# Taking the constant products out of the norm pauses of a two-block transformer kernel

## The chip, the cores and the metric

The kernel runs as one launch on one NeuronCore of a Trainium2 chip. The metric is the device time of the launch in microseconds (us); lower is better. TensorE (PE in the profile) does the matrix products, VectorE (DVE) and ScalarE (ACT) the elementwise work, GpSimd (POOL) and SyncE (SP) mostly start transfers.

## The reference

Two blocks of a network are run one after the other on 256 tokens of width 1024, all in float32.

The first block has two layers over a context and a latent sequence of 256 tokens each (512 columns together). Layer 0 is a retention mixer, layer 1 a differential attention mixer; each is followed by a gated feed-forward part of hidden width 2816. In front of every mixer and feed-forward part stands a modulated RMS norm:

```
def modulate(x, shift, scale):
    return rms_norm(x) * (1.0 + scale) + shift
```

The second block has two layers over the latent tokens. Each has a feed-forward part of hidden width 4096, a mixer with three branches (a gated delta rule and two kinds of chunked attention), and another feed-forward part; after each of the three stands a LayerNorm:

```
x = layer_norm(alpha * x + 0.5 * swiglu_2(x, w_ff1_in[l], w_ff1_out[l]), ln1_g[l], ln1_b[l])
...
x = layer_norm(alpha * x + mix, ln2_g[l], ln2_b[l])
x = layer_norm(alpha * x + 0.5 * swiglu_2(x, w_ff2_in[l], w_ff2_out[l]), ln3_g[l], ln3_b[l])
```

## The kernel before

**Products.** Every weight matrix is cut into tiles of 1 MB (16 blocks of 128x128). SP loads them through a ring of four buffers `raw`; ACT makes a rounded copy `w_hi` of each tile (ring of two), DVE the rest `w_lo`, in place of `raw`. Activations are split the same way. One float32 product is then three matmuls (high by high, high by low, low by high), in `product` (L444 to L446) and `product_rows` (L450 to L452). `wide_both` does it with two (L500 with 512 columns, L501 with 256). PE waits for `lo_done` at each tile and counts `tile_used` at its end; that count lets ACT and DVE go on with the tile after the next.

**Order of the work.** Each engine runs a program written out by hand, in order. The engines meet at semaphores only: an engine stands still at `wait_ge` until another has counted far enough.

**The pauses of the norms.** Between the last product of one part and the first product of the next lies a norm, and it needs the sum over all 1024 features. There are nine such pauses in which TensorE has constant products to do:

- Pause A, ahead of the first feed-forward part: sums of squares on TensorE (L601, L593), then ACT and DVE scale and split eight blocks of features, one after the other. `wide(..., blocks=...)` starts the next part block by block, as `block_ready` counts them.
- Pause B, ahead of the differential attention; the same, with 256 columns first.
- Pause C, ahead of the second feed-forward part; the same.
- Pause D, ahead of the second block: the residual is added and split, without a norm.
- Pauses E, five of them, in `turned_norm(n)` for n = 0 to 4 (the two layers have n % 3 = 0, 1, 2; the last norm of all doesn't go through TensorE). The tokens lie on the partitions there. DVE and ACT work out mean and deviation of the first 128 tokens, PE turns them with eight transposes (L642), then the same for the other 128 (L649); DVE and ACT scale and split the eight blocks, and the next part starts with block 0.

**The constant products.** `keep_clock(bank_, count)` issues `count` float32 matmuls of a matrix of ones with four constant 128x128 matrices, 512 columns each, into a PSUM bank that nothing reads before it is written anew. The profile has two instructions for each of them (L440). There are 1 and 5 in pause A, 4 in B, 4 in C, 4 in D, and 3, 1 and 1 in each pause E: ahead of the first transposes, between the two groups, and behind the second. They wait for nothing of their own. Those behind a `wait_ge` stand in order behind it.

Of the kernel before, what the change touches and what calls it, by code (L numbers as in the profile page):

```python
# [32 lines left out]
P = 128  # L33
# [60 lines left out]
def build(nc, ws, xt, col1, row1, col2, row2, relb, cst, ret_cst, ret_dist, c64, crow, aw, lnrow, out):  # L94
# [3 lines left out]
    def at(name, shape, kb, dtype=F32):  # L98
        return nc.alloc_sbuf_tensor_at(name, shape, dtype, offset=base + int(kb * KB) // 32 * 32)
# [13 lines left out]
    cs = at("cs", [P, 6, P], 96)  # L113
    ident, ones, ones64, rot_ret, rot_diff, swap64 = (cs[:, i, :] for i in range(6))
# [121 lines left out]
    with ExitStack() as ctx:  # L236
        ps = ctx.enter_context(nc.psum_tensor("ps", [P, 8, 512], F32))
# [62 lines left out]
        def tiles(phase, layer, eng, body, first=0, count=None, per=4):  # L300


            n0, _, total = PH[phase]
            count = total - first if count is None else count
            turns = count // per
            done = 0
            if turns > 1:
                with eng.Fori(0, turns) as i:
                    for u in range(per):
                        body(i, u, n0 + first + u, i * (per // 4) + layer * (NL // 4))  # L310
                done = turns * per
            for u in range(done, count):
                body(0, u, n0 + first + u, layer * (NL // 4))
# [9 lines left out]
        UNITS = [("q", 0), ("q", 1), ("ka", 0), ("kb", 0), ("ka", 1), ("kb", 1), ("va", 0), ("vb", 0), ("q", 2), ("ka", 2), ("kb", 2),  # L323
                 ("va", 1), ("vb", 1), ("q", 3), ("ka", 3), ("kb", 3), ("va", 2), ("vb", 2), ("va", 3), ("vb", 3)]
        UNIT_TILE = list(itertools.accumulate(0 if n == 0 or kind[1:] == "b" else 1 for n, (kind, _) in enumerate(UNITS)))
        DIFF_OUT_BANK = (0, 0, 1, 1, 4, 4, 5, 5)

# [102 lines left out]
        def _(pe):  # L430
            mm = nc.tensor.matmul

            def pass_wait():

                pe.sem_inc(waits_passed)

            def keep_clock(bank_, count):

                for _ in range(count):
                    mm(ps[:, bank_, :].rearrange("p (a b) -> p a b", b=P), ones, cs[:, 0:4, :], start=True, stop=True)  # L440

            def product(out_, blk, s, rhs_hi, rhs_lo, start, stop):

                mm(out_, w_hi[:, s % SPLIT, blk], rhs_hi, start=start, stop=False)  # L444
                mm(out_, w_hi[:, s % SPLIT, blk], rhs_lo, start=False, stop=False)  # L445
                return mm(out_, w_lo[:, raw_slot(s), blk], rhs_hi, start=False, stop=stop)  # L446
# [42 lines left out]
            def wide_both(phase, layer, rhs, first=0, count=None, blocks=None):  # L489

                def body(i, u, s, turn):
                    wait_tile(s, turn)
                    pe.wait_ge(sums_taken, group(phase, layer, i * 4 + first + u - 1))
                    for n in range(2 * DC):
                        c, mi = (n // 2, n % 2) if blocks is not None else (n % DC, n // DC)
                        if blocks is not None and mi == 0:
                            pe.wait_ge(block_ready, blocks + c + 1)
                            pass_wait()
                        o, blk = ps[:, ring(first + u) + mi, :], mi * DC + c
                        mm(o.rearrange("p (a b) -> p a b", b=T), w_hi[:, s % SPLIT, blk], rhs[:, :, c, :], start=c == 0, stop=False)  # L500
                        ins = mm(o[:, 0:T], w_lo[:, raw_slot(s), blk], rhs[:, 0, c, :], start=False, stop=c == DC - 1)  # L501
                    ins.then_inc(tile_used, 1)
                if blocks is not None:
                    pe.wait_ge(sums_taken, group(phase, layer, first + 2))
                    pass_wait()
                tiles(phase, layer, pe, body, first, count)
# [18 lines left out]
            def deep(phase, layer, rhs_hi, rhs_lo, width, parts, complete, early=None):  # L525


                def body(i, u, s, turn):
                    wait_tile(s, turn)
                    q = u % parts  # L530
                    if q == 0:
                        pe.wait_ge(sums_taken, group(phase, layer, u // parts + 1))
                    if u == parts - 1:
                        pe.wait_ge(operand_ready, complete)
                        pass_wait()
                    b = pair(phase, u // parts)
                    for mi in range(2):
                        if mi and early is not None:
                            early(u)
                        for c in range(DC):  # L540
                            ins = product(ps[:, b + mi, 0:width], mi * DC + c, s, rhs_hi[:, q * DC + c, :],
                                          rhs_lo[:, q * DC + c, :], q == 0 and c == 0, q == parts - 1 and c == DC - 1)
                    ins.then_inc(tile_used, 1)
                tiles(phase, layer, pe, body, per=4 * parts)
# [42 lines left out]
            def squares(q, cols, some, sq, bank_=5):  # L587

                width = cols.stop - cols.start
                for c in some:  # L590
                    pe.wait_ge(sq_ready, q * DC + c + 1)
                    pass_wait()
                    ins = mm(ps[:, bank_, 0:width], ones, sq[:, c, 0:width], start=c == 0, stop=c == DC - 1)  # L593
                if c == DC - 1:
                    ins.then_inc(square_sum, 1)

            def added_squares(q, width, sq, number):

                pe.wait_ge(sq_added, number)
                pass_wait()  # L600
                mm(ps[:, 5, 0:width], ones, sq[:, 0, 0:width], start=True, stop=False)  # L601
# [33 lines left out]

            def turned_norm(n):

                keep_clock(0 if n % 3 == 1 else 5, 3)
                pe.wait_ge(z_ready, n * 3 + 1)
                pass_wait()  # L640
                for c in range(DC):
                    nc.tensor.transpose(ps[:, 4 + 2 * (c % 2), (c // 2) * P:(c // 2 + 1) * P], x_tok[:, 0, c * P:c * P + P], ident)  # L642
                for c in (0, 2, 4, 6, 1, 3, 5, 7):
                    if c == 0:
                        keep_clock(5, 1)
                    if c < 2:
                        pe.wait_ge(z_ready, n * 3 + 2 + c)
                        pass_wait()
                    ins = nc.tensor.transpose(ps[:, 5 + 2 * (c % 2), (c // 2) * P:(c // 2 + 1) * P], x_tok[:, 1, c * P:c * P + P],  # L649
                                              ident)  # L650
                    if c in (6, 7):
                        ins.then_inc(z_turned, 1)
                keep_clock(3, 1)

            pe.sem_inc(tile_used, SPLIT)

# [77 lines left out]
            for j in range(16):  # L734
# [6 lines left out]
                for n, (kb, ka) in enumerate(keys):  # L741
                    ins = mm(ps[:, HO_BANK[j], :], att[:, h % 2, ka, (q % 2) * P:(q % 2) * P + P], V[:, h, kb, :],  # L742
                             start=n == 0, stop=n == len(keys) - 1)
# [6 lines left out]
            pe.wait_ge(ho_copied, 12)  # L750
            wide("ret_g", 0, h_hi, h_lo, TT, early=lambda u: (head_turned(14), head_turned(15)) if u == 0 else None)
            deep("ret_out", 0, y_hi, y_lo, TT, 2, 2)
            keep_clock(6, 1)
            added_squares(1, TT, SQ_RET, 1)
            squares(1, slice(0, TT), range(6, DC), SQ_RET)
            keep_clock(6, 5)
            wide("ffn_in0", 0, h_hi, h_lo, TT, 0, 4, blocks=DC)
            pe.wait_ge(operand_ready, 3)
            wide("ffn_in0", 0, h_hi, h_lo, TT, 4)
# [1 line left out]


            squares(2, slice(0, TT), range(5, DC), SQ_DIFF, 0)
            keep_clock(6, 4)

            def projection():

# [232 lines left out]
                    if j > 7:  # L1000
                        squares(3, LAT, (j // 2 - 5, j // 2 - 4), SQ_LAT, 7)
            squares(3, LAT, range(4, DC), SQ_LAT, 7)
            keep_clock(6, 4)
            wide_both("ffn_in1", 0, h_both[:, :, :, LAT], 0, 1, blocks=3 * DC)
            pe.wait_ge(operand_ready, 7)
            wide_both("ffn_in1", 0, h_both[:, :, :, LAT], 1, 1)
            wide_both("ffn_in1", 0, h_both[:, :, :, LAT], 2)
            ffn_out("ffn_out1", slice(0, T), 8)
            pe.wait_ge(x_ready, DC + 1)
            keep_clock(0, 4)  # L1010


            for layer in range(LAYERS2):
# [14 lines left out]
                wide_both("ff1_in", layer, l_both, 4)  # L1028
                ff_out("ff1_out", "ff1_in", layer, layer * 7 + 10)
                turned_norm(layer * 3)  # L1030
                wide("w_in", layer, l_hi, l_lo, T, 0, 4, blocks=layer * 3 * DC + 5 * DC)
                have(2)
# [165 lines left out]
                for lv in range(6):  # L1198
                    for g in range(2):
                        pe.wait_ge(inv_ready, layer * 12 + lv * 2 + g + 1)  # L1200
                        pass_wait()
                        for y, half, h, n in systems(range(4 * g, 4 * g + 4)):
                            rhs = TU[half, g, 0, y % 4, :] if lv else m64[half, 9, :]
                            ins = mm(ps[half, 4 + 3 * g, (y % 4) * CH:(y % 4 + 1) * CH], Mm[half, y, :], rhs,
                                     start=True, stop=True)
                        ins.then_inc(inv_p, 1)
                    products(3)
                    for g in range(2):
# [4 lines left out]
                        for y, half, h, n in systems(range(4 * g, 4 * g + 4)):  # L1213
                            p, u, at_ = Pm[half, y, :], TU[half, g, 1, y % 4, :], y % 4
# [17 lines left out]
                for y, half, h, n in systems(range(8)):  # L1232
                    ins = mm(ps[:, 4 + h // 2, y * CH:y * CH + CH], kbg[half, y, :], TU[half, y // 4, 1, y % 4, :],
                             start=True, stop=True)
# [3 lines left out]
                for n in range(4):  # L1238
                    if n:
                        pe.wait_ge(sc_next, layer * 3 + n)  # L1240
                        pass_wait()
                        for j, hp, half, h in heads:
                            ins = mm(ps[half, 2, j * P:j * P + P], wT[:, 8 * hp + 4 * j + n, :], Sst[:, n % 2, h, :],
                                     start=True, stop=True)
# [4 lines left out]
                    if n < 3:  # L1249
                        for j, hp, half, h in heads:  # L1250
                            ins = mm(ps[:, 6 + hp, j * P:j * P + P], kdec[half, 4 * j + n, :], vnew[half, n % 2, j, :],
                                     start=True, stop=True)
# [4 lines left out]
                    for j in range(2):  # L1257
                        outs = [ps[:, 3 + 2 * hp, j * T + n * CH:j * T + n * CH + CH] for hp in range(2)]
                        for hp, half in enumerate(HALVES):
                            if n:  # L1260
                                mm(outs[hp], Sst[:, n % 2, 2 * hp + j, :], qdec[:, 8 * hp + 4 * j + n, :],
                                   start=True, stop=False)
                        for hp, half in enumerate(HALVES):
                            ins = mm(outs[hp], vnew[half, n % 2, j, :], qkT[half, 4 * j + n, :],
                                     start=n == 0, stop=True)
# [1880 lines left out]
```

## Time and profile before

| | |
|---|---|
| median of 3 runs | 2979.86 us (2979.3 to 2986.58) |
| time of the profiled execution | 2979.24 us |
| its span, first to last instruction | 2977.4 us |
| PE busy | 2922.7 us, 98% |
| weight loads on PE | 2486.7 us, 84% |
| DVE busy | 1978.0 us, 66% |
| ACT busy | 1269.8 us, 43% |
| mean granted TensorE clock | 0.999 of full speed |

Busy times are sums over the instructions of an engine. A matmul's record reaches a little beyond the start of the next one, since matmuls are pipelined; how fast they follow each other is read from their starts. The granted clock is given as a share of 2.4 GHz: 1.00 is 2.4 GHz and 0.50 is 1.2 GHz.

### The profile page before, as it was taken

The numbers are of one execution on the slowest core, as the hardware profiler recorded it, in microseconds if no ns is written. First come the engines' busy times: TensorE is split into PE (matmuls) and PEld (weight loads), VectorE is DVE, ScalarE is ACT, GpSimd is POOL, SyncE is SP. The second block draws the span as 40 slices with busy tenths as digits, with TensorE's granted clock in tenths as the row PEclk, the third lists the DMA queues.
The fourth block names the chain that finished last, engine by engine and source line by source line (L and its number), as shares of the span: only waits on it lengthen the run. The fifth ranks groups of instructions, "written<-read, shape, count | busy, mean of one in ns | idle before, by whom it ended". The sixth has DMA issues, their size and how long they took to land.

```text
span 2977.4 us, 45013 instructions
## 1 busy us (share of the span) xinstructions
PE 2922.7 (98%) x17734; PEld 2486.7 (84%) x17734; DVE 1978.0 (66%) x2717; ACT 1269.8 (43%) x1469; POOL 25.0 (1%) x36
## 2 busy tenths in 40 slices
PE   8999999999999999999999999999999999999998
PEld 5896887888877788988889988888888899988887
DVE  5754656766656767477557867775677478777764
ACT  5312224222154465344443635554544345536553
POOL 0000000000000000010000000000100000000000
PEclk9999999999999999999999999999999999999999
DMA  7430343444522145455545324555555544335554
GB/s 296 156 128 15 134 149 134 163 170 161 191 90 71 57 144 195 169 199 194 200 171 183 143 86 162 188 187 185 184 192 188 210 160 169 104 138 180 187 183 169
DMA packets 71595, 475.35 MB, mean 160 GB/s; under 512 B 8065, under 2 KB 8225, under 8 KB 19745
## 3 DMA queue, kind: packets, MB, share of 16 engines
q1 hardware_dynamic: 57744, 418.47, 39.2%
q10 hardware_dynamic: 11520, 41.95, 4.2%
q0 software_dynamic: 2192, 12.96, 1.1%
q8 instruction: 102, 1.67, 0.2%
q14 instruction: 37, 0.30, 0.0%
HBM read 472.31 MB, written 1.05 MB: 159 GB/s over the span
## 4 chain that ended last, share of the span: by engine, by line
PE 91%; DVE 5%; ACT 2%; DVEq 1%; issue 1%; DMA 0%; ACTq 0%; SPq 0%
PE ps L500 18%; PE ps L444 12%; PE ps L445 12%; PE ps L446 12%; PE ps L501 9%; PE ps L450 6%; PE ps L451 6%; PE ps L452 6%; DVE w_lo L1878 2%; PE ps L742 1%; PE ps L712 1%; PE ps L440 1%; PE ps L816 1%; ACT w_hi L1314 0%; DMA raw<-in_ws 0%
## 5 line engine op out<-in xcount | busy, mean ns | idle before, releaser
L1878 DVE TENSOR_TENSOR w_lo<-raw,w_hi 128x2048 fp32r<-128x2048 f32 x369 | 846.0, 2293 | 497.1 <-ACT w_hi L1314 495.5
L1314 ACT CAST w_hi<-raw 128x2048 fp32r<-128x2048 f32 x367 | 700.5, 1909 | 658.4 <-PE ps L446 325.0
L500 PE MATMUL ps<-l_both,w_hi 128*128 128x512 f32 x2048 | 718.5, 396 | 4.4 <-DVE small L2053 2.4
L501 PE MATMUL ps<-l_both,w_lo 128*128 128x256 f32 x2048 | 572.7, 280 | 0.0
L500 PEld LDWEIGHTS ps<-l_both,w_hi 128*128 128x128 f32 x2048 | 384.1, 188 | 100.4 <-issue 6.5
L501 PEld LDWEIGHTS ps<-l_both,w_lo 128*128 128x128 f32 x2048 | 386.4, 189 | 0.0
L444 PE MATMUL ps<-h_both,w_hi 128*128 128x512 f32 (+1 forms) x736 | 285.8, 388 | 3.4 <-DVE h_both L2142 2.1
L446 PE MATMUL ps<-h_both,w_lo 128*128 128x512 f32 (+1 forms) x736 | 279.8, 380 | 0.0
L445 PE MATMUL ps<-h_both,w_hi 128*128 128x512 f32 (+1 forms) x736 | 279.7, 380 | 0.0
L444 PE MATMUL ps<-l_both,w_hi 128*128 128x256 f32 x848 | 247.7, 292 | 2.7 <-DVE w_lo L1932 1.2
L1435 ACT COPY low_part<-ps 128x512 f32<-128x512 f32 x150 | 88.1, 587 | 369.5 <-PE ps L501 369.5
L446 PE MATMUL ps<-l_both,w_lo 128*128 128x256 f32 x848 | 239.8, 283 | 0.0
L445 PE MATMUL ps<-l_both,w_hi 128*128 128x256 f32 x848 | 239.8, 283 | 0.0
L450 PE MATMUL ps<-w_hi,fh_hi 128*128 128x512 f32 x512 | 199.2, 389 | 0.0
L452 PE MATMUL ps<-w_hi,fh_lo 128*128 128x512 f32 x512 | 199.2, 389 | 0.0
L451 PE MATMUL ps<-w_lo,fh_hi 128*128 128x512 f32 x512 | 199.2, 389 | 0.0
L444 PEld LDWEIGHTS ps<-h_both,w_hi 128*128 128x128 f32 x736 | 138.3, 188 | 39.2 <-issue 12.3
L444 PEld LDWEIGHTS ps<-l_both,w_hi 128*128 128x128 f32 x848 | 162.3, 191 | 10.4 <-issue 6.1
L445 PEld LDWEIGHTS ps<-l_both,w_hi 128*128 128x128 f32 x848 | 162.4, 192 | 0.6 <-issue 0.5
L446 PEld LDWEIGHTS ps<-l_both,w_lo 128*128 128x128 f32 x848 | 162.3, 191 | 0.0
L445 PEld LDWEIGHTS ps<-h_both,w_hi 128*128 128x128 f32 x736 | 138.4, 188 | 26.8 <-issue 1.7
L446 PEld LDWEIGHTS ps<-h_both,w_lo 128*128 128x128 f32 x736 | 138.3, 188 | 26.5
(468 smaller groups left out, 5006.3 us busy)
## 6 DMA issues: line engine op xcount, KB each, us to landing
raw<-in_ws SPq DMA_DIRECT2D x396, 1024.0 KB, 4.8
aT<-in_aw ACTq DMA_DIRECT2D x80, 512.0 KB, 4.1
ln_rows<-in_lnrow POOLq DMA_DIRECT2D x4, 1024.0 KB, 6.1
X<-in_xt SPq DMA_DIRECT2D x1, 2048.0 KB, 11.2
dist<-in_ret_dist POOLq DMA_DIRECT2D x1, 2048.0 KB, 14.8
relB<-in_relb POOLq DMA_DIRECT2D x2, 768.0 KB, 7.3
c_rows<-in_crow POOLq DMA_DIRECT2D x1, 1024.0 KB, 9.0
last_rows<-in_lnrow POOLq DMA_DIRECT2D x1, 1024.0 KB, 5.9
```

What stands on the lines that cost most here:

```text
L440: mm(ps[:, bank_, :].rearrange("p (a b) -> p a b", b=P), ones, cs[:, 0:4, :], start=True, stop=True)
L444: mm(out_, w_hi[:, s % SPLIT, blk], rhs_hi, start=start, stop=False)
L445: mm(out_, w_hi[:, s % SPLIT, blk], rhs_lo, start=False, stop=False)
L446: return mm(out_, w_lo[:, raw_slot(s), blk], rhs_hi, start=False, stop=stop)
L450: mm(out_, x_hi, w_hi[:, s % SPLIT, blk], start=start, stop=False)
L451: mm(out_, x_hi, w_lo[:, raw_slot(s), blk], start=False, stop=False)
L452: return mm(out_, x_lo, w_hi[:, s % SPLIT, blk], start=False, stop=stop)
L500: mm(o.rearrange("p (a b) -> p a b", b=T), w_hi[:, s % SPLIT, blk], rhs[:, :, c, :], start=c == 0, stop=False)
L501: ins = mm(o[:, 0:T], w_lo[:, raw_slot(s), blk], rhs[:, 0, c, :], start=False, stop=c == DC - 1)
L1314: nc.scalar.copy(w_hi[:, s % SPLIT], raw[:, raw_slot(s)]).then_inc(hi_done, 1)
L1435: nc.scalar.copy(low_part[:, own], ps[:, b:b + 2, T:TT]).then_inc(low_ready, 1)
L1878: tt(w_lo[:, raw_slot(s)], raw[:, raw_slot(s)], w_hi[:, s % SPLIT].bitcast(F32), ALU.subtract).then_inc(lo_done, 1)
```

## The change

All calls of `keep_clock` go, and the function with them. Nothing is put in their place; all waits, all other instructions and their order stay.

```diff
--- before.py
+++ after.py
@@ -434,11 +434,6 @@
 
                 pe.sem_inc(waits_passed)
 
-            def keep_clock(bank_, count):
-
-                for _ in range(count):
-                    mm(ps[:, bank_, :].rearrange("p (a b) -> p a b", b=P), ones, cs[:, 0:4, :], start=True, stop=True)
-
             def product(out_, blk, s, rhs_hi, rhs_lo, start, stop):
 
                 mm(out_, w_hi[:, s % SPLIT, blk], rhs_hi, start=start, stop=False)
@@ -635,14 +630,11 @@
 
             def turned_norm(n):
 
-                keep_clock(0 if n % 3 == 1 else 5, 3)
                 pe.wait_ge(z_ready, n * 3 + 1)
                 pass_wait()
                 for c in range(DC):
                     nc.tensor.transpose(ps[:, 4 + 2 * (c % 2), (c // 2) * P:(c // 2 + 1) * P], x_tok[:, 0, c * P:c * P + P], ident)
                 for c in (0, 2, 4, 6, 1, 3, 5, 7):
-                    if c == 0:
-                        keep_clock(5, 1)
                     if c < 2:
                         pe.wait_ge(z_ready, n * 3 + 2 + c)
                         pass_wait()
@@ -650,7 +642,6 @@
                                               ident)
                     if c in (6, 7):
                         ins.then_inc(z_turned, 1)
-                keep_clock(3, 1)
 
             pe.sem_inc(tile_used, SPLIT)
 
@@ -750,10 +741,8 @@
             pe.wait_ge(ho_copied, 12)
             wide("ret_g", 0, h_hi, h_lo, TT, early=lambda u: (head_turned(14), head_turned(15)) if u == 0 else None)
             deep("ret_out", 0, y_hi, y_lo, TT, 2, 2)
-            keep_clock(6, 1)
             added_squares(1, TT, SQ_RET, 1)
             squares(1, slice(0, TT), range(6, DC), SQ_RET)
-            keep_clock(6, 5)
             wide("ffn_in0", 0, h_hi, h_lo, TT, 0, 4, blocks=DC)
             pe.wait_ge(operand_ready, 3)
             wide("ffn_in0", 0, h_hi, h_lo, TT, 4)
@@ -761,7 +750,6 @@
 
 
             squares(2, slice(0, TT), range(5, DC), SQ_DIFF, 0)
-            keep_clock(6, 4)
 
             def projection():
 
@@ -1000,14 +988,12 @@
                     if j > 7:
                         squares(3, LAT, (j // 2 - 5, j // 2 - 4), SQ_LAT, 7)
             squares(3, LAT, range(4, DC), SQ_LAT, 7)
-            keep_clock(6, 4)
             wide_both("ffn_in1", 0, h_both[:, :, :, LAT], 0, 1, blocks=3 * DC)
             pe.wait_ge(operand_ready, 7)
             wide_both("ffn_in1", 0, h_both[:, :, :, LAT], 1, 1)
             wide_both("ffn_in1", 0, h_both[:, :, :, LAT], 2)
             ffn_out("ffn_out1", slice(0, T), 8)
             pe.wait_ge(x_ready, DC + 1)
-            keep_clock(0, 4)
 
 
             for layer in range(LAYERS2):
```

## Rows read from the trace of the kernel before

**Rows 1.** The page: busy times, granted clock, and the shares of the last-ending chain.

```profile
PE 2922.7 (98%) x17734; PEld 2486.7 (84%) x17734; DVE 1978.0 (66%) x2717; ACT 1269.8 (43%) x1469; POOL 25.0 (1%) x36
...
PEclk9999999999999999999999999999999999999999
...
PE 91%; DVE 5%; ACT 2%; DVEq 1%; issue 1%; DMA 0%; ACTq 0%; SPq 0%
```

**Rows 2.** The constants' line: duration in ns (min/median/max), first and last start.

```profile
L440 PE MATMUL ps<-cs x86: 590/592/596, 471.6 to 2696.9; 128*128 128x512 f32 x86
```

**Rows 3.** Timeline of PE, pause A and its last two blocks (start, us, instructions).

```profile
471.58 1.02 PE L440 MATMUL ps<-cs 128*128 128x512 f32 x2
472.44 1.02 PE L601 MATMUL ps<-SQ_RET,cs 128*128 128x512 f32 x2
474.25 1.95 PE L593 MATMUL ps<-SQ_RET,cs 128*128 128x512 f32 x4 [0.79 <-ACT SQ_RET L1340]
476.04 4.45 PE L440 MATMUL ps<-cs 128*128 128x512 f32 x10
481.20 0.47 PE L444 MATMUL ps<-h_both,w_hi 128*128 128x512 f32 x1 [0.70 <-DVE h_both L1939]
...
491.17 0.47 PE L444 MATMUL ps<-h_both,w_hi 128*128 128x512 f32 x1
...
492.39 0.39 PE L446 MATMUL ps<-h_both,w_lo 128*128 128x512 f32 x1
492.85 0.47 PE L444 MATMUL ps<-h_both,w_hi 128*128 128x512 f32 x1
```

**Rows 4.** Timeline of PE, pause B.

```profile
850.23 3.60 PE L440 MATMUL ps<-cs 128*128 128x512 f32 x8
853.96 0.36 PE L444 MATMUL ps<-h_both,w_hi 128*128 128x256 f32 x1
```

**Rows 5.** Timeline of PE, pause C.

```profile
1068.86 3.60 PE L440 MATMUL ps<-cs 128*128 128x512 f32 x8
1073.63 0.47 PE L500 MATMUL ps<-h_both,w_hi 128*128 128x512 f32 x1 [1.17 <-DVE h_both L1939]
```

**Rows 6.** Timeline of PE, pause D.

```profile
1265.01 3.60 PE L440 MATMUL ps<-cs 128*128 128x512 f32 x8
1269.26 0.47 PE L500 MATMUL ps<-l_both,w_hi 128*128 128x512 f32 x1 [0.65 <-DVE l_both L2564]
```

**Rows 7.** Timeline of PE, the first of the five pauses E.

```profile
1535.95 2.73 PE L440 MATMUL ps<-cs 128*128 128x512 f32 x6
1538.70 1.06 PE L642 MATMUL ps<-cs,x_tok 128*128 128x128 f32 x8
1539.60 1.02 PE L440 MATMUL ps<-cs 128*128 128x512 f32 x2
1540.66 1.08 PE L649 MATMUL ps<-cs,x_tok 128*128 128x128 f32 x8
1541.59 1.02 PE L440 MATMUL ps<-cs 128*128 128x512 f32 x2
1543.00 0.36 PE L444 MATMUL ps<-l_both,w_hi 128*128 128x256 f32 x1 [0.39 <-DVE l_both L2034]
```

**Rows 8.** Timeline of DVE in that pause: what frees PE.

```profile
1537.74 0.81 DVE L1998 TENSOR_SCALAR x_tok<-x_tok,negmu,inv_std 128x1024 f32<-128x1024 f32 x1 [0.24 <-ACT inv_std L1378]
...
1539.97 1.00 DVE L2020 TENSOR_SCALAR x_tok<-x_tok,negmu,inv_std 128x512 f32<-128x512 f32 x2 [0.64 <-ACT inv_std L1388]
1541.34 0.54 DVE L2026 TENSOR_SCALAR X<-ps,cols 128x256 f32<-128x256 f32 x1 [0.36 <-PE ps L649]
```

**Rows 9.** Timeline of PE at the second tile behind pauses E, n = 0.

```profile
1549.58 0.39 PE L444 MATMUL ps<-l_both,w_hi 128*128 128x256 f32 x1 [0.59 <-DVE w_lo L1932]
```

**Rows 10.** The same for n = 1.

```profile
1852.10 0.48 PE L500 MATMUL ps<-l_both,w_hi 128*128 128x512 f32 x1 [1.21 <-DVE small L2053]
```

**Rows 11.** Timeline of PE at the kernel's start: one form of matmul.

```profile
6.59 4.35 PE L678 MATMUL ps<-raw,cond_raw 128*4 128x256 f32 x10 [6.59 <-DMA raw<-in_ws]
...
10.38 1.86 PE L678 MATMUL ps<-raw,cond_raw 128*4 128x256 f32 x7
15.47 1.89 PE L678 MATMUL ps<-raw,cond_raw 128*4 128x256 f32 x8 [3.23 <-DMA raw<-in_ws]
17.30 0.60 PE L663 MATMUL ps<-parts_sum,ada_row 4*128 4x2 f32 x4
```

**Rows 12.** Stretches: length, each engine's busy us (instructions), granted clock, DMA.

```profile
10.00:15.00 5.00, 2.24 (x9) 0.66 (x7) 1.25 (x3) 2.06 (x4) 0.00 (x0) 1.00 0.99 420
...
2967.80:2970.00 2.20, 0.00 (x0) 0.00 (x0) 2.07 (x4) 1.57 (x5) 0.00 (x0) 1.00 0.00 0
2970.20:2972.00 1.80, 0.00 (x0) 0.00 (x0) 1.65 (x5) 0.50 (x2) 0.00 (x0) 0.50 0.00 0
```

**Rows 13.** Timeline of PE: its last matmul.

```profile
2967.34 0.39 PE L452 MATMUL ps<-w_hi,fh_lo 128*128 128x512 f32 x1
```

## The prediction

> **What bounds the kernel now.** I read the page first. TensorE is busy for 98% of the span and makes up 91% of the chain that ended last, and its granted clock reads 9 (90% or more) in all forty slices [rows 1]. So the kernel is bound by TensorE at full clock, and whatever slows the products there goes into the time nearly one for one. Next I asked for the line of the constants: 86 instructions, 590 to 596 ns each, spread from 471.6 to 2696.9 us [rows 2]. Then I read the timeline of PE around each of their places. In pause A the ten instructions of the second call start at 476.04 and the next follows 4.45/10, about 0.43 us, behind each; the 86 fill some 37 us of TensorE. The question is only whether these 37 us stand in for idle time, and what idle time would do instead. Last I looked for places where TensorE's clock changes without the constants: only the two ends of the kernel have such rows.
>
> **What goes.** 43 calls, 86 instructions. Each stands ahead of a wait that ends later than they do. Pause A: they run from 476.04 to 480.5 and the next product starts at 481.20, when DVE has released it (0.70 us idle left) [rows 3]; pause C leaves 1.17 us [rows 5], pause D 0.65 [rows 6]. Pause B has the least room, but the row behind it shows the product at 853.96, 0.13 us behind the end of the last constant's record [rows 4]; its operand came at about that time. In pause E the first transpose starts at 1538.70, and DVE wrote its operand until 1537.74 + 0.81 = 1538.55; the second group starts at 1540.66, and half of the 1.00 us of DVE's two instructions that began at 1539.97 ends at 1540.5 [rows 7, 8]. So in both places TensorE starts 0.15 us behind the operand, constants or not. The cover of the whole edit is this: the norm's chain on ACT and DVE, which has nothing to do with the constants. Taking them out gives back nothing directly. Bounds: at best 0.15 us at each of ten transpose groups and at pause B, 1.6 us; at worst a start from standstill is later. The first product of pause C comes 0.26 us behind its block, as do those of A and D, against 0.15 in E, so a loss of 0.1 at six places, 0.6 us. I take 0.4 us of loss.
>
> **What is idle then.** Pause A: 472.5 to 474.25, and 476.0 to 481.20 (5.2 us) [rows 3]. B: 850.2 to 853.96 (3.7 us) [rows 4]. C: 4.8 us [rows 5]. D: 4.3 us [rows 6]. E: 2.75 us, eight transposes (0.9 us), 1.06 us, eight transposes, 1.4 us [rows 7]; that is 5.2 idle of 7.05, five times over.
>
> **What the clock does in idle time.** The end of the kernel shows it: the last matmul starts at 2967.34 and its record ends at 2967.73 [rows 13]; the granted clock is 1.00 until 2970.00 and 0.50 from 2970.20 on [rows 12]. So 2.4 us behind the last product the clock was at 1.2 GHz. Against that, TensorE was idle for 3.23 us up to 15.47 and the clock stayed at 1.00 [rows 11, 12]. So idle time of this size sometimes brings the clock down and sometimes not; pauses A, C and D are longer than either, B is a little longer, and E is made of pieces around it. I take it that the clock falls in A, C and D, nearly always in B, and in most of the five E.
>
> **What a fallen clock costs.** The start shows both levels for one form of matmul. The first ten start from 6.59 to 10.38, 3.79/9 = 0.42 us apart; the eight from 15.47 to 17.30 are 1.83/8 = 0.23 us apart [rows 11]. At the low level work takes 1.84 times as long, so each us of it loses 0.46 us. There the high level came at about 10.7, some 4.1 us behind the first matmul. If a pause's products run that long at 1.2 GHz, it loses 4.1 x 0.46 = 1.9 us. But the fall comes during the pause, and part of the low stretch lies in idle time; then half, 0.95 us, is left. Between the two I take 1.4 us, since the products start only when the norm is over and the low stretch has to last into them.
>
> **What of it is absorbed.** Behind A, B and C the blocks arrive more slowly than PE takes them. In A a block comes every 492.85 - 491.17 = 1.68 us, and its work ends at 492.39 + 0.23, 1.45 us after its start [rows 3]: 0.23 us to spare in each of seven, 1.6 us in all. For B and C I take 1.1 and 1.4 us from the same blocks at 256 columns (0.16 and 0.20 each). D has no such room. E with n = 0 and 3 waits 0.59 us for the second tile's weights [rows 9], n = 1 and 4 wait 1.21 us [rows 10], n = 2 doesn't wait. These waits are for ACT's and DVE's work on tiles that TensorE has released earlier, so they don't move with it.
>
> Loss less absorption, with 1.4 us a pause: A 0, B 0.3, C 0, D 1.4, E 0.8 x 2 + 0.2 x 2 + 1.4 = 3.4. Sum 5.1 us. With 1.9 us: A 0.3, B 0.8, C 0.5, D 1.9, E 1.3 x 2 + 0.7 x 2 + 1.9 = 5.9. Sum 9.4. With 0.95 us: D 0.95, E 0.35 x 2 + 0.95 = 1.65. Sum 2.6.
>
> **Transposes at the low clock.** The chain of E runs through TensorE: DVE starts on block 0 at 1541.34, 0.7 us behind the first transpose of the second group [rows 7, 8], after four of its eight. Eight take 0.9 us; four take 0.45, and at the low clock 0.38 more. That is late for all that follows, for nothing is absorbed ahead of it: 5 x 0.38 = 1.9 us if the clock falls before them each time, 0 if never. I take half, 1.0 us.
>
> On this the Trainium skill has a rule that speaks against my middle value (TensorE: Matmul & The Clock Gate, Part 4: PE-mode transpose): full speed doesn't engage for transposes as it does for other matmuls. No run here shows it yet; by it each E would be one pause of 7.05 us and the clock would fall ahead of the second group every time, and the sum would be the third rival's.
>
> **Sum.** 5.1 + 1.0 + 0.4 = 6.5 us. The profiled execution took 2979.24 us, 1.84 more than its span; it lies 0.6 us below the median of the runs. 2979.24 + 6.5 = 2985.7; with half of the distance to the median, 2986. That is 0.2%, and a measurement of this kernel tells about 0.3%, 8.9 us, from no change.
>
> **Rivals.**
>
> First, the clock falls in most pauses and the loss is partly absorbed: my forecast, 2982 to 2988.8. Chance 0.47.
>
> Second, the clock doesn't fall, or only where it costs nothing. The 3.23 us of idleness at full clock [rows 11, 12] speak for it, the last 2.4 us [rows 12, 13] against. Time: 2979.9. Chance 0.11.
>
> Third, the transposes don't hold the clock up, and all five E run from their first transposes into their products at 1.2 GHz. E costs 5.9 + 1.9 us, A to D 1.7 (0.3 and 1.4, as above), the slower starts 0.6: 10.1 us, 2989.3, and so slower. For it: 5.2 of 7.05 us are idle in each E. Against it: only 2.75 us lie in one piece. It decides from the point at which the five E together cost more than 6.5 us. Chance 0.24.
>
> Fourth, nothing is absorbed, since the slack is taken up by ACT and DVE, whose next tiles wait for `tile_used`, and each pause costs the full 1.9 us: 9 x 1.9 + 1.9 + 0.6 = 19.6 us, 2998.8; in between, with half absorbed, 2994. For it: all ring buffers hang on TensorE's progress. Against it: rows 9 and 10 are waits for tiles that are free already when the pause starts. Chance 0.15.
>
> Fifth, the constants hold real work up, and it gets faster: at most the 1.6 us above, since their ends lie ahead of what they stand before. Reaching 0.3% would need 8.9. Chance 0.03 for all that would do this.
>
> **How the numbers follow.** The forecast is the likeliest case, 2986. Cases one and two are within 0.3%: 0.47 + 0.11 = 0.58. Three and four are slower: 0.39. Faster: 0.03. The range goes from the second rival, 2979.5, to half absorption in the fourth, 2994, and leaves out some 0.12.
>
> **What the profile after would show.** No L440. The granted clock below 1.00 in short stretches at some of the nine pauses, five to nine of them, each some us long. Directly behind A, B and C first products twice as far apart as now, and the last blocks on time. The waits of rows 9 and 10 shorter, by what the products lost. In E the second group of transposes longer than 1.08 us in some pauses, and DVE's first instruction behind it later. The prediction is wrong if the clock stays at 1.00 (then 2979.9), or if it takes more than 4.1 us of products in a pause to come back (then it costs up to twice as much), or if a later wait of another engine is set off.

## The result, and the profile after

The changed kernel takes 2991.78 us (median of 20 runs, 2985.56 to 2997.78), the kernel before on the same chip 2985.99 us (median of 20, 2978.93 to 2991.99). The ratio is 1.0022, with a 95% interval of 1.0014 to 1.003. On 2980 us that is 6.6 us more (4.2 to 8.9). Differences in us of a comparison are the ratio's here and below; they need not be those of the medians, which are 5.8 us apart here. The forecast was 6.5 us more, as a time 2986 us in a range of 2979.5 to 2994.

The profiled execution of after took 2991.7 us with a span of 2989.9, 12.5 us more span than that of before. The page, with the lines that answer to [rows 1]:

```profile
PE 2904.5 (97%) x17648; PEld 2490.5 (83%) x17648; DVE 1978.1 (66%) x2717; ACT 1270.0 (42%) x1469; POOL 23.3 (1%) x36
...
PEclk9999999999999999999999999999999999999999
...
PE 90%; DVE 5%; ACT 2%; DVEq 1%; issue 1%; DMA 0%; ACTq 0%; SPq 0%
```

PE has 86 instructions and 18 us of busy time less, not the 37 us that the constants filled: other products, at the low clock, took longer. The row of the clock can't tell this; it reads 9 for anything from 0.90 up. The mean over the span does: 0.990 after, 0.999 before. So the clock has to be read in stretches of a few us. Windows of the profile after (columns as in [rows 12]), a row or two for each pause, in order: A (two), B, C, D, the five E (n = 0 to 4, two rows for n = 2), and last three stretches that lie in no pause:

```profile
481.26:484.10 2.84, 2.84 (x7) 2.26 (x8) 2.07 (x4) 2.71 (x7) 0.00 (x0) 0.50 0.00 0
484.10:494.50 10.40, 10.30 (x44) 7.73 (x43) 5.68 (x10) 8.90 (x16) 0.00 (x0) 1.00 0.19 63
852.70:859.60 6.90, 5.61 (x26) 5.64 (x27) 4.77 (x13) 6.46 (x15) 0.00 (x0) 0.51 0.00 0
1074.60:1078.00 3.40, 3.40 (x11) 2.83 (x11) 2.67 (x8) 3.21 (x8) 0.00 (x0) 0.50 0.00 0
1272.60:1276.00 3.40, 3.40 (x13) 2.92 (x12) 2.38 (x2) 1.25 (x1) 1.67 (x4) 0.50 0.69 170
1536.00:1547.30 11.30, 6.57 (x37) 5.05 (x35) 9.27 (x24) 6.80 (x16) 0.00 (x0) 1.00 0.52 186
1849.40:1856.20 6.80, 5.43 (x19) 4.61 (x20) 5.14 (x13) 4.55 (x11) 0.00 (x0) 0.50 0.03 13
2122.50:2125.80 3.30, 3.04 (x14) 2.70 (x15) 1.64 (x7) 2.10 (x5) 0.00 (x0) 0.50 0.60 251
2126.00:2127.40 1.40, 0.34 (x4) 0.11 (x1) 1.25 (x4) 0.95 (x3) 0.00 (x0) 1.00 0.00 0
2402.40:2409.20 6.80, 5.95 (x28) 5.58 (x28) 5.11 (x14) 4.66 (x13) 0.00 (x0) 0.50 0.00 0
2706.20:2713.00 6.80, 5.08 (x18) 4.26 (x19) 4.96 (x12) 4.73 (x11) 0.00 (x0) 0.50 0.11 46
1781.20:1784.50 3.30, 3.30 (x20) 2.93 (x19) 0.00 (x0) 0.00 (x0) 0.00 (x0) 0.50 0.31 124
1811.90:1815.20 3.30, 3.30 (x18) 3.30 (x17) 3.23 (x3) 0.00 (x0) 0.00 (x0) 0.50 0.27 109
2668.70:2672.00 3.30, 3.30 (x18) 3.30 (x17) 3.13 (x3) 0.00 (x0) 0.00 (x0) 0.50 0.40 164
```

The clock fell to 1.2 GHz in eight of nine pauses; the exception is E with n = 0. The low stretches last about 3.4 or 6.8 us. The last three rows are falls without a pause of a norm; that before has such falls too is shown below. The timeline of PE after, at pauses A and D and at E with n = 1 and 2:

```profile
481.26 0.76 PE L439 MATMUL ps<-h_both,w_hi 128*128 128x512 f32 x1 [5.00 <-DVE h_both L1925]
481.83 0.63 PE L440 MATMUL ps<-h_both,w_hi 128*128 128x512 f32 x1
...
492.90 0.47 PE L439 MATMUL ps<-h_both,w_hi 128*128 128x512 f32 x1
...
1272.22 0.47 PE L495 MATMUL ps<-l_both,w_hi 128*128 128x512 f32 x1 [4.05 <-DVE l_both L2550]
1272.52 0.36 PE L496 MATMUL ps<-l_both,w_lo 128*128 128x256 f32 x1
1272.69 0.63 PE L495 MATMUL ps<-l_both,w_hi 128*128 128x512 f32 x1
1273.12 0.41 PE L496 MATMUL ps<-l_both,w_lo 128*128 128x256 f32 x1
1273.33 0.63 PE L495 MATMUL ps<-l_both,w_hi 128*128 128x512 f32 x1
...
1847.91 1.06 PE L636 MATMUL ps<-cs,x_tok 128*128 128x128 f32 x8 [2.53 <-DVE x_tok L1984]
1849.88 1.94 PE L641 MATMUL ps<-cs,x_tok 128*128 128x128 f32 x8 [0.90 <-DVE x_tok L2006]
1852.71 0.77 PE L495 MATMUL ps<-l_both,w_hi 128*128 128x512 f32 x1 [0.89 <-DVE l_both L2020]
...
2122.74 1.94 PE L636 MATMUL ps<-cs,x_tok 128*128 128x128 f32 x8 [2.53 <-DVE x_tok L1984]
2124.70 1.64 PE L641 MATMUL ps<-cs,x_tok 128*128 128x128 f32 x8
2127.50 0.47 PE L495 MATMUL ps<-l_both,w_hi 128*128 128x512 f32 x1 [1.16 <-DVE l_both L2020]
```

Pause A [rows 3]: the first product starts at 481.26 (481.20 before), the idle time ahead of it is 5.00 us instead of 0.70, and the next product starts 0.57 us behind it. At 492.90 the last block is 0.05 us late (492.85 before), no more than the products ahead of the pause are (0.06 us): here the fall cost nothing. Pause D [rows 6]: the clock falls with the third product at 1272.69, and two matmuls together take 0.64 us (1272.69 to 1273.33) where the same two take 0.35 in before (1270.04 to 1270.39, below), with no slack behind them. Pause E with n = 1: the second group of transposes takes 1.94 us where [rows 7] has 1.08. The two rows of before for pause D:

```profile
1270.04 0.40 PE L500 MATMUL ps<-l_both,w_hi 128*128 128x512 f32 x1
...
1270.39 0.40 PE L500 MATMUL ps<-l_both,w_hi 128*128 128x512 f32 x1
```

**The price of each pause.** I took the start of one and the same instruction ahead of a pause and some tiles behind it in both traces; what it comes later than in before, in us, is the price. In brackets: us at 1.2 GHz around that pause. Besides after, the traces of four experiments that are told below:

| | A | B | C | D | E0 | E1 | E2 | E3 | E4 | sum |
|---|---|---|---|---|---|---|---|---|---|---|
| after | 0 (3.4) | 0.73 (6.8) | 0.05 (3.4) | 1.48 (3.4) | 0 (0) | 0.85 (6.8) | 0.61 (3.4) | 1.37 (6.8) | 0.86 (6.8) | 5.9 |
| the change again | 0 (3.4) | 1.01 (6.8) | 0.05 (3.4) | 1.47 (3.4) | 1.81 (10.2) | 0.86 (6.8) | 0.89 (3.4) | 1.39 (6.8) | 0.85 (6.8) | 8.3 |
| two columns | 0 (6.8) | 0 (3.4) | 0.83 (6.8) | 1.53 (3.4) | 0 (0) | 0.84 (6.8) | 0.05 (0) | 1.05 (6.8) | 0.76 (3.4) | 5.1 |
| E alone | | | | | 0.93 (6.8) | 0.85 (3.4) | 0.05 (0) | 1.37 (6.8) | 0.76 (6.8) | 4.0 |
| A to D alone | 0 (3.4) | 0 (3.4) | 0.49 (6.8) | 1.43 (3.4) | | | | | | 1.9 |

Of the 12.5 us between the two profiled spans, the pauses make 5.9, the three other falls 1.5 + 1.4 + 1.4 = 4.3, and the pace of the products of `wide_both` 2.1 (told below). Together 12.3. As far as the traces below show, only the first of the three follows from the change; the medians, which differ by less, average over the other two.

### The profile page after: what moved, and what is told of

The parts are those of the page before. It is cut to its first block, busy times and chain, and to the rows that moved or that the text cites. A ratio compares the mean times of both kernels' runs of the same rounds, so it can differ in the third digit from the quotient of the medians.

```text
span 2989.9 us, 44841 instructions
## 1 busy us (share of the span) xinstructions
PE 2904.5 (97%) x17648; PEld 2490.5 (83%) x17648; DVE 1978.1 (66%) x2717; ACT 1270.0 (42%) x1469; POOL 23.3 (1%) x36
## 3 DMA queue, kind: packets, MB, share of 16 engines
HBM read 472.31 MB, written 1.05 MB: 158 GB/s over the span
## 4 chain that ended last, share of the span: by engine, by line
PE 90%; DVE 5%; ACT 2%; DVEq 1%; issue 1%; DMA 0%; ACTq 0%; SPq 0%
PE ps L495 19%; PE ps L439 12%; PE ps L441 12%; PE ps L440 12%; PE ps L496 9%; PE ps L445 6%; PE ps L446 6%; PE ps L447 6%; DVE w_lo L1864 2%; PE ps L733 1%; PE ps L703 1%; DVE w_lo L1918 1%; PE ps L804 1%; ACT w_hi L1300 0%; DMA raw<-in_ws 0%
```

## Experiments

**Without the constants of pauses E alone.**

```diff
 def turned_norm(n):
-    keep_clock(0 if n % 3 == 1 else 5, 3)
     pe.wait_ge(z_ready, n * 3 + 1)
...
-        if c == 0:
-            keep_clock(5, 1)
...
-    keep_clock(3, 1)
```

> Constants taken out of the five pauses E alone, kept in A to D. Theory of the prediction (the clock falls in most of them, later waits absorb a part): the E terms of the sum, 3.4 for the products, 1.0 for transposes at the low clock, 0.2 for later starts, 4.6 us, a ratio of 1.0015, with the granted clock at 0.50 in three to five of the five E and nowhere in A to D. Third rival (transposes don't hold the clock up, all five fall ahead of the second group): 5.9 + 1.9 + 0.4 = 8.2 us, 1.0027. Second rival (no fall that costs): 0. The trace of the change adds a doubt: its 12.5 us over the profile of before contain about 4 us of falls outside of all pauses, at 1781, 1812 and 2669 us; if those come from the change, they are gone or fewer here.

Measured: 2989.88 us (11 runs) against 2982.80 for before (35 runs on this chip), ratio 1.0019 (1.0009 to 1.0029), or 5.7 us (2.7 to 8.7); mean clock over the runs 0.992, before's 0.998. In the trace four of the five pauses fell, none of A to D, and the five cost 4.0 us (table). So most of the change's loss comes from E (3.7 of 5.9 us in the trace of after). The interval holds the 4.6 us expected and the third rival's 8.2 us alike, so this run doesn't tell the two apart. Falls outside the pauses are there too, at 15.1, 1810.5 and 2670.7 us.

**Without the constants of pauses A to D alone.**

```diff
-keep_clock(6, 1)
 added_squares(1, TT, SQ_RET, 1)
 squares(1, slice(0, TT), range(6, DC), SQ_RET)
-keep_clock(6, 5)
...
 squares(2, slice(0, TT), range(5, DC), SQ_DIFF, 0)
-keep_clock(6, 4)
...
 squares(3, LAT, range(4, DC), SQ_LAT, 7)
-keep_clock(6, 4)
...
 pe.wait_ge(x_ready, DC + 1)
-keep_clock(0, 4)
```

> Constants taken out of pauses A to D alone, kept in the five E. Theory of the prediction: A 0, B 0.3, C 0, D 1.4 and 0.2 for later starts, 1.9 us, a ratio of 1.0006, with the granted clock at 0.50 in A, C and D and mostly B, and A's and C's last blocks on time again. Fourth rival (nothing absorbed): 4 x 1.9 = 7.6 us, 1.0026. Second rival: 0.

Measured: 2984.99 us, ratio 1.0007 (0.9998 to 1.0016), 2.1 us; in the trace 1.9 us, 1.43 of it in D. The fourth rival's 1.0026 lies outside the interval: it is out. Within the sum, B cost 0 and C 0.49 in this trace, where 0.3 and 0 were expected. The two halves add up to 5.7 + 2.1 = 7.8 us against 6.6 for the whole, the same within the intervals.

**Instructions without work.** The 86 instructions stay in their places but are two columns wide.

```diff
-mm(ps[:, bank_, :].rearrange("p (a b) -> p a b", b=P), ones, cs[:, 0:4, :], start=True, stop=True)
+mm(ps[:, bank_, 0:2], ones, cs[:, 0, 0:2], start=True, stop=True)
```

> All 43 constant products stay in place as instructions, but each has 2 columns in place of 512, so that the array has next to nothing to do. If it is the array's idleness that brings the clock down and costs the time, this is as slow as the change itself: 6.5 us, 1.0022, with the clock at 0.50 in most pauses. If TensorE only needed instructions in its queue, or if the price of the change were the start from standstill, this is within 1 us of before and the clock stays at 1.00.

Measured: 2991.29 us, ratio 1.003 (1.0019 to 1.0041), mean clock 0.989, as slow as the change itself. (Its profiled execution was the fastest of its 11, 2980.65 us: the quicker pace told below gave back about as much as its pauses cost.) Its timeline of PE in pause C, beside [rows 5]:

```profile
1069.10 0.95 PE L440 MATMUL ps<-cs 128*128 128x2 f32 x8
1073.86 0.77 PE L500 MATMUL ps<-h_both,w_hi 128*128 128x512 f32 x1 [3.81 <-DVE h_both L1939]
```

and its window there:

```profile
1073.00:1079.60 6.60, 5.74 (x18) 4.90 (x19) 4.65 (x12) 6.16 (x15) 0.00 (x0) 0.50 0.00 0
```

All eight instructions are there; they take 0.95 us instead of 3.60, and the clock falls. So it isn't the absence of instructions that costs, but the time in which the array does next to nothing.

**Transposes in place of the constants.** Each float32 constant of 512 columns becomes eight transposes of 128, about as long.

```diff
-mm(ps[:, bank_, :].rearrange("p (a b) -> p a b", b=P), ones, cs[:, 0:4, :], start=True, stop=True)
+for k in range(8):
+    nc.tensor.transpose(ps[:, bank_, (k % 4) * P:(k % 4 + 1) * P], ones, ident)
```

> Each of the 43 constant products becomes eight 128x128 transposes of constants into the same bank, which fill about the same time (eight transposes took 0.9 us, one constant product 0.86 us). If transposes hold the granted clock up as the products do, this is before: ratio 1.000, no fall in the nine pauses. If they don't (the Trainium skill, TensorE: Matmul & The Clock Gate, Part 4), the clock falls in all nine pauses as without constants, and the time is that of the change, 1.002, or more. A middle is open: a transpose might count for less than a product.

Measured: 2986.72 us (12 runs) against 2984.68 for before (23 runs on this second chip), ratio 1.0008 (0.9999 to 1.0018), mean clock 0.997, before's 0.9975. Its windows around A, B, D and E0 (those around the other five also read 1.00):

```profile
472.00:495.00 23.00, 21.21 (x105) 14.92 (x104) 14.57 (x23) 19.07 (x32) 0.00 (x0) 1.00 0.23 82
849.00:862.00 13.00, 12.91 (x87) 10.47 (x86) 9.63 (x22) 10.71 (x23) 0.67 (x2) 1.00 0.26 101
1262.00:1280.00 18.00, 17.37 (x126) 16.08 (x125) 13.27 (x22) 9.50 (x13) 3.71 (x7) 1.00 0.64 223
1532.00:1556.00 24.00, 22.98 (x175) 21.41 (x174) 18.45 (x40) 13.01 (x26) 0.00 (x0) 1.00 0.34 130
```

No fall in any of the nine pauses, where nearly everything that PE did was transposes. They hold the clock at 2.4 GHz as the constants do, and the third rival has lost its mechanism.

**Half of the constants.** One call's count of 3 becomes 1 in E (1, 1 and 1), 5 becomes 2 in A, 4 becomes 2 in B, C and D: 24 of the 43 are left.

```diff
-keep_clock(0 if n % 3 == 1 else 5, 3)
+keep_clock(0 if n % 3 == 1 else 5, 1)
...
-keep_clock(6, 5)
+keep_clock(6, 2)
...
-keep_clock(6, 4)
+keep_clock(6, 2)
...
-keep_clock(0, 4)
+keep_clock(0, 2)
```

> Fewer constants: 1, 1 and 1 in each pause E (before 3, 1, 1), 1 and 2 in A (1, 5), 2 in each of B, C and D (4). That leaves about 1.7 us more idle time in each E, 2.6 in A, 1.7 in B, C and D. By my reading of before (a gap of 2.4 us at the kernel's end brought the clock down, one of 3.2 us at its start did not), the clock falls in some of the pauses only: ratio between 1.0000 and 1.0015, mean clock between those of before (0.998) and the change (0.989). If half is enough everywhere, it is 1.000 and no fall in the nine.

Measured: 2985.21 us, ratio 0.9999 (0.9989 to 1.001), mean clock 0.996. Windows in A, B, D and E0:

```profile
481.10:484.40 3.30, 2.90 (x7) 2.35 (x8) 2.53 (x5) 3.17 (x7) 0.00 (x0) 0.50 0.00 0
850.00:857.00 7.00, 5.14 (x24) 3.08 (x22) 5.84 (x13) 6.54 (x14) 0.00 (x0) 1.00 0.38 153
1273.00:1276.20 3.20, 3.20 (x12) 2.71 (x11) 2.45 (x2) 0.54 (x1) 0.96 (x2) 0.50 0.89 250
1535.00:1552.00 17.00, 14.83 (x87) 11.54 (x86) 13.74 (x34) 11.77 (x25) 0.00 (x0) 1.00 0.38 123
```

The clock fell in A, C and D, and of these only D cost anything (1.49 us in the trace). In B and all five E the half was enough in this execution. In time it can't be told from before.

**More constants.** PE waits twice for up to 1.84 us ahead of `have(3)`, in the second block's branch outputs; constants were put there.

```diff
+    keep_clock(6, 2)
     have(3)
     tiles("w_br", layer, pe, branch, 4, 2)
```

> Nothing taken out; two more constant products in each layer of the second block, ahead of the wait for the gated delta rule's output (TensorE stands there for 1.84 us in both layers of before). If falls of the clock at that place belong to the kernel before as well, and come and go from one execution to the next, this saves their price of about 1.5 us in the executions that had them: 0.5 to 2 us faster in the median, 0.9995. If those falls come only with the change, there is no difference. If the two constants (1.7 us) hold the branch products up, it is slower by up to 0.2 us a layer.

Measured: 2985.73 us (12 runs), ratio 1.0006 (0.9995 to 1.0016), mean clock 0.998, which is before's too. The profiled execution, the fastest of the twelve, had no fall outside the two ends, and a span of 2974.1 us, but the median shows nothing of the 0.5 to 2 us expected.

**Both kernels a second time, for the trace.** The kernel before and the changed one, unedited, one profiled execution each on the second chip.

> The kernel before once more, for a second trace. Its runs have mean clocks of 0.996 to 0.999, so falls outside of the pauses should belong to it too: one or two of 3.4 us, at the gated delta rule or the branches (1781, 1811, 2661 to 2670 us in the other traces). If none is there in a run with a clock of 0.998 or less, falls come from elsewhere. The pitch of the alternating 512- and 256-column products (346.8 or 353.5 ns for a pair, per part of the kernel) should again differ from part to part.

> The change once more, for a second trace: how many of the nine pauses the clock falls in, and what each costs. Expected from the first one: 1.4 to 1.5 us in D whenever it falls, 0 in A, 0 to 0.7 in B, 0 to 0.8 in C, 0 to 1.4 in each E, with one or two of the E without a fall.

Before took 2990.87 us (span 2989.1, mean clock 0.997), 11.6 us more than its first profiled execution. Its windows:

```profile
1207.20:1210.40 3.20, 3.20 (x17) 3.20 (x16) 0.73 (x3) 0.00 (x0) 0.00 (x0) 0.50 0.00 0
1814.80:1818.10 3.30, 3.30 (x17) 3.30 (x17) 3.21 (x3) 0.00 (x0) 0.00 (x0) 0.50 0.31 132
2668.10:2671.40 3.30, 3.30 (x17) 3.30 (x17) 3.06 (x4) 0.00 (x0) 0.00 (x0) 0.50 0.60 251
15.90:19.20 3.30, 3.30 (x9) 0.96 (x8) 3.06 (x6) 1.51 (x3) 0.00 (x0) 0.50 1.01 427
```

Three falls behind waits between products, one at the kernel's start behind a wait for weights, none in the nine pauses. One or two were expected. So falls outside the pauses belong to the kernel before as well, from execution to execution, and aren't the change's. The changed kernel took 2997.47 us (mean clock 0.989): all nine pauses fell this time, for 8.3 us, and three other places (the start at 15.4, then 1817.6 and 2674.4 us). B with 1.01 and the first E with 1.81 us cost more than the 0.7 and 1.4 expected at most, and one or two E without a fall had been expected.

No version was found that is faster than both kernels.

## Why the prediction was right

The difference came out within 0.1 us of the sum (6.6 against 6.5), but that closeness is luck: the interval runs from 4.2 to 8.9 us, and two terms were off in opposite directions. More was lost at the low clock than forecast, and more of it was absorbed. In the trace of after, PE's records fill 35 of the 41 us that the pauses ran at 1.2 GHz; at 0.46 us each that is an estimated 16 us of loss, of which 5.9 stayed. The forecast has 9 x 1.4 + 1.0 = 13.6 us with the transposes, of which 6.1 stay. As a time the forecast was 5.8 us low (2986 against 2991.78), because it started from one execution of before at 2979.24, and the 20 runs of before have a median of 2985.99.

**What goes.** Right. Taking the constants out gave nothing back directly. The later starts, for which I had taken 0.4 us, measured about 0: the first product of A comes 0.06 us later, as late as what stands ahead of the pause, and the other starts aren't late either.

**Where the clock falls.** Right for A, C and D, and for B: 16 falls in the 16 pauses A to D of the four traces without full constants there (after, again, two columns, A to D alone). Of the E pauses 16 of 20 fell, "most of the five".

**Loss and absorption, A to D.** Predicted 0, 0.3, 0 and 1.4, together 1.7. Measured 0, 0.7 to 1.0, 0.05 and 1.48 in the two traces of the changed kernel, together 2.3 and 2.5. D is the clearest: 3.4 us at 1.2 GHz by the 0.46 us of [rows 11] is 1.56, and 1.43 to 1.53 were lost. B was mis-sized: I had one loss for all pauses, but its low stretch lasted 3.4 us in two traces (price 0) and 6.8 in two, and there it outran the slack. In after B's products ran at 1.2 GHz from 853.99 to 859.6, 5.6 us, an estimated 2.6 us of loss, and 0.73 stayed: some 1.8 us were absorbed, where I had taken 1.1. C is alike: 0.05 us with 3.4 us low, 0.83 and 0.49 with 6.8. The slack in A (1.6 us) held in every trace, though twice as many us were low in one of them.

**A sign of being wrong that came.** The prediction named as one that it takes more than 4.1 us of products in a pause for the clock to come back. It did in B (the 5.6 us above), and in E with n = 0 of the second trace the clock was low for 10.2 us; at 1.81 us that is the dearest pause of all. The 4.1 us, read at the kernel's start, was too short for the pauses; that this didn't show in the sum is part of the luck.

**E.** Predicted 3.4 for the products and 1.0 for the transposes, 4.4; the measured sums over the five are 3.7, 5.8, 2.7 and 4.0 in the four traces of the table that have them, mean 4.0. The split was wrong. The mis-sized term is "Transposes at the low clock". I had taken DVE's path alone, which needs four of the second eight transposes; but ACT takes block 1 and needs all eight. The row of ACT after, and under it that of before, at n = 1:

```profile
1851.86 0.56 ACT L1382 ACTIVATE X<-ps,cols 128x256 f32<-128x256 f32 x1 [1.77 <-PE ps L641]
```

```profile
1843.83 0.56 ACT L1396 ACTIVATE X<-ps,cols 128x256 f32<-128x256 f32 x1 [0.92 <-PE ps L649]
```

ACT starts 1.98 us behind the first transpose of the group (1849.88) after, 1.13 before (1842.70): 0.85 us late, and E1 costs 0.85 in all. DVE's first instruction, at 1851.01 behind 1849.88, comes 1.13 us behind instead of 0.67. At n = 2 the second group takes 0.56 us longer than in [rows 7] and the price is 0.61. At n = 3 and 4 the second group takes 0.75 and 0.86 us longer. So the transposes and the chain behind them carry most of the loss of such a pause, 0.86 + 0.56 + 0.75 + 0.86 = 3.0 us over the four E that fell in after instead of 1.0, and the products' own loss is nearly all absorbed; some 0.6 us of it stays at n = 3 (1.37). The waits that were to absorb it did: those of rows 9 and 10 are gone at n = 1, 3 and 4 of after, and the one at n = 0, which didn't fall, is there with 0.6 us.

**The rivals.** The second (no fall) is refuted by the eight pauses at 0.50. Its evidence, 3.23 us of idleness at full clock at the kernel's start, didn't hold from one execution to the next: at the same place the second execution of before fell behind 2.13 us of it. The fourth (nothing absorbed, 19.6 us) lies far above the interval, and is refuted by A to D alone, and by the pauses A and C of after that fell and cost 0 and 0.05 us. For the third (transposes don't hold the clock), whose 10.1 us lie above the interval of 4.2 to 8.9, two rows decide. In the windows above, 2122.50 to 2125.80 is at 0.50 and 2126.00 to 2127.40 at 1.00, and between the last product, which starts at 2119.83, and 2127.50 PE did nothing but sixteen transposes: the clock rose on transposes alone. The kernel with transposes in place of constants shows that they also keep it up. By the rule of the Trainium skill (TensorE: Matmul & The Clock Gate, Part 4: PE-mode transpose) full speed shouldn't engage for them; the figures that it gives there are for bf16. For this form (float32, 128 by 128) this case's runs disagree: ratio 1.0008 and mean clock 0.997, where the change has 1.0022 and 0.989. The measurement decides. The fifth (faster) had nothing for it.

**What the low clock costs over all.** The runs give the sum over many executions. Mean clock 0.9892 over the 20 runs of after, 0.9980 over 35 of before: 0.0088 of 2980 us, at half speed, is 26.2 / 0.5 = 52 us more at 1.2 GHz. They cost 6.6 us, 13%, where 0.46 for each us of work would be 24 us. Little of the rest lay in idle time (6 of 41 us in the trace of after); most was paid from waits that come later anyway. That absorption, not the fall, was what the forecast hung on.

**What was not foreseen.** The falls outside the pauses and the two paces (below) moved the profiled execution by 6 us, as much as the change, without being caused by it. In 35 runs of before, the 11 with a mean clock of 0.999 average 2979.7 us, the 15 with 0.998 2983.0, the 8 with 0.997 2987.3 (the one with 0.996 took 2981.9). This is also why the range was better taken around a ratio than around a time.

## What to carry to other kernels

Idle TensorE time in which the clock may fall has a price at each place of its own: find who waits for the first instructions behind the pause, and how much slack the rest has. Here pauses with blocks that arrive slowly (A, C) cost nothing as long as the low stretch was short (3.4 us), one with products back to back (D) cost 1.5 us, and those with a short chain through TensorE (transposes that ACT and DVE wait for) cost the chain's delay, 0.6 to 0.9 us, or more. So constants have most to save in the latter two kinds; a kernel with constants there alone was not run. When one piece of work feeds two engines, follow both to the one that starts last.

## What the runs showed of the hardware that wasn't expected

**Two paces of the same products.** In `wide_both` a matmul of 512 columns and one of 256 alternate, at full granted clock and without waits. A pair takes 346.7 ns in one part of an execution and 353.3 in another, measured between distant starts; which part has which changes from execution to execution, and costs about 3.4 us for a part of 512 pairs. The number of 512-column matmuls in three such parts shows it, in the windows of that line alone: before,

```profile
1100.00:1180.00 80.00, 80.00 (x232) 1.00 0.55 195
1900.00:2000.00 100.00, 100.00 (x284) 1.00 0.52 187
2180.00:2280.00 100.00, 100.00 (x290) 1.00 0.53 189
```

after,

```profile
1100.00:1180.00 80.00, 80.00 (x227) 1.00 0.52 185
1900.00:2000.00 100.00, 100.00 (x289) 1.00 0.53 189
2180.00:2280.00 100.00, 100.00 (x284) 1.00 0.52 185
```

Before is quick, slow, quick; after is slow, quick, slow; the second execution of before had slow, slow, quick. All of it is at 1.00. What sets the pace stays open: no run was made for it.

**Which idle times bring a fall.** In the pauses A to D without constants, or with two-column ones, the clock fell each time, in E, with its idleness in pieces, 16 times of 20. At the kernel's start it fell behind idle pieces of 2.13 to 2.65 us in four of the ten traces, and in six it didn't, behind 1.61 to 3.23 us. Outside the pauses one and the same wait brings a fall in one execution and none in another. The timeline of PE at it, after:

```profile
1810.36 0.36 PE L439 MATMUL ps<-o_hi,w_hi 128*128 128x256 f32 x1 [1.85 <-DVE mrt L2831]
```

and before, with the window behind it:

```profile
1804.59 0.35 PE L444 MATMUL ps<-o_hi,w_hi 128*128 128x256 f32 x1 [1.84 <-DVE mrt L2845]
```

```profile
1804.60:1815.00 10.40, 10.40 (x87) 10.40 (x88) 9.64 (x10) 3.08 (x4) 0.00 (x0) 1.00 0.53 192
```

After, the clock was at 0.50 from 1811.90 on, and so was that of the second execution of before from 1814.80 on; in the first execution of before it stayed at 1.00. So the length of the idle piece alone doesn't decide it.
